# GpSimd's work in a diffusion layer moved to VectorE, behind ScalarE's rounding

## The chip, the core and the metric

One core of a Trainium2 chip runs the whole layer as one program. The metric is the device time of one execution in microseconds. The kernel before takes 2390.72 us, the median of 3 runs (2388.92 to 2391.03).

## The reference, cut to what matters

One layer of a hybrid diffusion backbone over 512 latent tokens and 256 context tokens, width 2048, everything in float32:

```
x  = x + grid_pos_embed
sh1, sc1, gt1, sh2, sc2, gt2 = split(silu(c) @ w_ada + b_ada)      # the ada matrix: 2048 x 12288
hx = rms_norm(x) * (1 + sc1) + sh1                                 # the same for the context, with c_ctx
u_f, u_x, u_g = split(hx @ w_in)
y_lru     = (forward + backward RG-LRU of conv(u_x)) * gelu(u_g)   # 8 heads of 128
y_fourier = real(fft2(u_f)) @ w_fourier + b                        # 4 groups of 256
x  = x + gt1 * rms_norm(concat(y_fourier, y_lru) @ w_out)
h2 = rms_norm(x) * (1 + sc2) + sh2
g, v = split(conv(h2 @ w_up))                                      # 2 x 5632 wide, 3 taps
x  = x + gt2 * rms_norm((gelu(g) * v) @ w_down)
```

## The kernel before

**Number format.** Activations and weights are cut in two parts so that float32 products can be made by three faster matmuls: hi is the value rounded to fp32r, lo is the value less hi. A product is hi x hi + hi x lo + lo x hi (`three`, L709 to L713).

**The weight stream.** All large weights come as 344 units of 128x1024 in the order of their use. A ring of four slots holds a unit three times: `w_raw` (what the DMA brought), `w_hi` (ScalarE, `round_unit`, L437 to L441) and `w_lo` (GpSimd, `remainders`, L391 to L396). Four units are a round. TensorE waits for `lo_done` before a unit. The semaphore `hi_done` counts ScalarE's roundings, and `lo_done` also frees `w_raw`: SP loads the next unit into a slot when the slot's last lo part is done (`load_unit`, L280). All loads go through SP's one queue, in the order of the code.

**The ada matrix.** The first 4096 columns are multiplied by TensorE at the start (L722 to L731, 0 to 135 us). The rest, 32 chunks of 256 columns, is worked out on VectorE beside the other work: `eat_ada` (L1017 to L1037) does one chunk as 16 steps `ada_acc = rows * scale + ada_acc` over 128x256, in pairs per load of 128x512, with four slots for the loads (`load_ada`, L288: a load waits until the slot was eaten). TensorE then sums `ada_acc` over the partitions (`sum_ada`, L779), and `take_ada` (L1011) adds the bias.

**The stages.** (1) TensorE's ada columns, the norms, and h in hi and lo (L1079 to L1106). (2) Eight heads (PE L787, ACT L499, DVE L1147): for head h TensorE makes u_x with units 0 and 1 of round h, and u_g with units 2 and 3, then the gates from `xc`. VectorE convolves, splits `xc`, takes the last ada chunk, finishes the head before, eats the next chunk, and works out the gap of the recurrence. ScalarE rounds units 0 and 1 of round h + 1 after the seeds of the convolution, and 2 and 3 after the exponentials. (3) Four Fourier groups (L871, L553, L1183), two ada chunks each. (4) The output projection, 16 tiles of two units (L908, L609, L1289); beside it one ada chunk per tile. After each tile ScalarE rounds two units of the next round. During the last half of this stage GpSimd adds the positions to x1 (eight additions of 128x1024, L405). (5) Between the halves: x1 is made from y (L1312 to L1319, 16 tiles: a scaling on VectorE, then a sum; GpSimd has 11 of the sums, in `POOL_SUM`), its squares are summed, h2 is made in hi and lo (L1323 to L1332; GpSimd has 5 of the 16 tiles, `POOL_H2`), and a last ada chunk but one is eaten. (6) The FFN in 11 chunks of 4 pairs: a pair is four units (g, then v), a down projection eight units; VectorE adds convolution taps (L1338, L1341), splits the activations (L1346), multiplies (L1358) and adds the down tiles (L1365). (7) The last norm and sum (L1396 to L1403; GpSimd has 11 of the 16 sums) and the stores.

**Who orders what.** Every engine has one list of instructions, written out by hand, and works through it in order. A wait stands in the list and holds back all that follows it on that engine. GpSimd's list has little beside `remainders`, so it stands waiting for `hi_done` and starts at once.

Of the kernel before, what the change touches and what calls it, by code (L numbers as in the profile page):

```python
# [21 lines left out]
F32 = mybir.dt.float32  # L22
# [7 lines left out]
KT = D // P  # L30
# [69 lines left out]
def build(nc, x_t, ctx_t, par_d, late_d, stream, ada0, adabg, gates_d, tabs_d, out_t):  # L100
    ctx = ExitStack()
    with ctx:
# [95 lines left out]
        with ExitStack() as s:  # L198
# [39 lines left out]
        y_normed, x1_done, x1_squared, x1_summed = (  # L238
            sem("y_normed"), (sem("x1_dve"), sem("x1_pool")), sem("x1_squared"), sem("x1_summed"))
        h2_pre, h2_rounded, h2_ready = ((sem(n + "_dve"), sem(n + "_pool")) for n in ("h2_pre", "h2_rounded", "h2_ready"))  # L240
# [4 lines left out]
        f_normed, out_ready, stored = sem("f_normed"), (sem("out_dve"), sem("out_pool")), sem("stored")  # L245
# [15 lines left out]

        POOL_SUM = [k for k in range(KT) if k % 3 != 2]
        POOL_H2 = [k for k in range(KT) if k % 3 == 2]

        def shared(sems, pool_tiles, k):

            mine = k in pool_tiles
            return sems[mine], sum((j in pool_tiles) == mine for j in range(k + 1))

# [9 lines left out]
        def _(sp):  # L279
# [103 lines left out]
            for k in range(KT):  # L383
                sp.wait_ge(*shared(out_ready, POOL_SUM, k))
                sp.dma_start(out_t[:, k, :], x1[:, k, :]).then_inc(stored, 16)
            sp.wait_ge(stored, 16 * KT)


        @block.gpsimd
        def _(pool):  # L390
            def remainders(r, slots=range(RING)):  # L391
                for s in slots:

                    pool.wait_ge(hi_done, r * RING + s + 1)
                    nc.gpsimd.tensor_tensor(w_lo[:, s, :], w_raw[:, s, :], w_hi[:, s, :].bitcast(F32),  # L395
                                            ALU.subtract).then_inc(lo_done, 1)  # L396

            with pool.Fori(0, R_OUT + 5) as r:
                remainders(r)

            pool.wait_ge(late_in, 16)
            for i in range(4):
                pool.wait_ge(x_in[i], 32)
                for half in range(2):
                    nc.gpsimd.tensor_tensor(*positions(x1, late_par, 4 * i + 2 * half, 2), ALU.add).then_inc(x_posed, 1)  # L405
                    if i + half < 4:
                        remainders(R_OUT + 5 + i, (2 * half, 2 * half + 1))

            for n, k in enumerate(POOL_SUM):
                pool.wait_ge(y_normed, n + 1)  # L410
                nc.gpsimd.tensor_tensor(x1[:, k, :], x1[:, k, :], tile(acc, k), ALU.add).then_inc(x1_done[1], 1)
            remainders(R_FFN, (2, 3))

            pool.wait_ge(rms_done, 4)
            for n in range(len(POOL_H2) + 1):
                if n < len(POOL_H2):
                    k = POOL_H2[n]
                    nc.gpsimd.tensor_tensor(tile(acc, k), x1[:, k, :], ss1[:, :], ALU.mult).then_inc(h2_pre[1], 1)
                if n > 0:
                    k = POOL_H2[n - 1]  # L420
                    pool.wait_ge(h2_rounded[1], n)
                    nc.gpsimd.tensor_tensor(h_lo[:, k, :], tile(acc, k), h_hi[:, k, :].bitcast(F32),
                                            ALU.subtract).then_inc(h2_ready[1], 1)
            with pool.Fori(R_FFN + 1, ROUNDS) as r:
                remainders(r)

            for n, k in enumerate(POOL_SUM):
                pool.wait_ge(f_normed, n + 1)
                nc.gpsimd.tensor_tensor(x1[:, k, :], x1[:, k, :], tile(acc, k), ALU.add).then_inc(out_ready[1], 1)
# [1073 lines left out]
```

## Time and profile before

| | us |
|---|---|
| median of 3 runs | 2390.72 |
| lowest, highest run | 2388.92, 2391.03 |
| profiled execution, span | 2397.1 |
| TensorE busy | 2224.0 |
| VectorE busy | 1170.5 |
| ScalarE busy | 717.5 |
| GpSimd busy | 918.3 |

The profile is of one execution of its own, and gives its span, from the first to the last instruction; its time isn't listed beside it, and the span stands 6.4 us above the median of the runs. PE is TensorE, DVE VectorE, ACT ScalarE, POOL GpSimd, SP the queue that issues the loads. Busy times of matmuls overlap, so a busy TensorE is not one at its peak. PEclk is the granted clock of TensorE as a share of 2.4 GHz; it has two levels, 2.4 and 1.2 GHz.

### The profile page before, as it was taken

To read this page: it belongs to the slowest core of one execution; us is meant where nothing else is said; L and a number is where in the kernel's file an instruction comes from. 1 tells how busy PE (TensorE), PEld (TensorE's weight loads), DVE (VectorE), ACT (ScalarE), POOL (GpSimd) and SP (SyncE) were. 2 spreads that over 40 slices of the span, in tenths; PEclk is the share of its full clock that TensorE was granted. 3 is DMA by queue.
4 is the path that set the end of the run, shared out by engine and by line. 5 is a ranking of instruction groups with operands and counts; after the bars stand their busy time and mean duration, and the time that the engine had idled before them with its cause. 6 is when DMAs were issued, how large, how long until landed. Compare 5 with 4: busy or idle time off the path is not lost.

```text
span 2397.1 us, 27540 instructions
## 1 busy us (share of the span) xinstructions
PE 2224.0 (93%) x9640; PEld 1750.7 (73%) x9640; DVE 1170.5 (49%) x1548; ACT 717.5 (30%) x938; POOL 918.3 (38%) x388
## 2 busy tenths in 40 slices
PE   8999989788888857999999999999999999999994
PEld 1268878677766626888888888888888888888883
DVE  4478888887788987323222222323232222223237
ACT  2345565422221233222222222222222222222222
POOL 0023222222234554444444444444444444444443
PEclk9999999888998978999999999999999999999997
DMA  9863424354476623323222222323232222223221
GB/s 347 277 206 112 148 82 142 134 169 145 137 249 231 210 75 105 105 88 103 90 97 96 95 97 88 104 87 105 88 101 91 96 96 93 99 88 104 87 87 70
DMA packets 102135, 301.50 MB, mean 126 GB/s; under 512 B 11344, under 2 KB 11344, under 8 KB 100816
## 3 DMA queue, kind: packets, MB, share of 16 engines
q1 hardware_dynamic: 102096, 300.99, 37.8%
q8 instruction: 23, 0.38, 0.1%
q14 instruction: 16, 0.13, 0.0%
HBM read 296.76 MB, written 4.19 MB: 126 GB/s over the span
## 4 chain that ended last, share of the span: by engine, by line
PE 69%; DVE 21%; DMA 5%; issue 3%; ACT 2%; DVEq 0%; POOL 0%; SPq 0%; ACTq 0%; POOLq 0%
PE bank L711 21%; PE bank L712 21%; PE bank L713 21%; DVE ada_acc L1033 10%; PE bank L729 4%; DMA ada_raw<-in_adabg 3%; DMA w_raw<-in_ada 1%; DVE xc L1120 1%; DVE ada_acc L1027 1%; DVE lru_i L1162 1%; DVE acc L1313 1%; DVE lru_i L1130 1%; DVE lru_u L1166 1%; DVE acc L1397 1%; DVE lru_u L1139 1%
## 5 line engine op out<-in xcount | busy, mean ns | idle before, releaser
L395 POOL TENSOR_TENSOR w_lo<-w_raw,w_hi 128x1024 fp32r<-128x1024 f32 x344 | 847.6, 2484 | 1411.0 <-ACT w_hi L441 1411.0
L711 PE MATMUL bank<-h_hi,w_hi 128*128 128x512 f32 x2048 | 814.4, 398 | 15.4 <-DVE h_lo L1331 9.4
L712 PE MATMUL bank<-h_lo,w_hi 128*128 128x512 f32 x2048 | 810.2, 396 | 0.0
L713 PE MATMUL bank<-h_hi,w_lo 128*128 128x512 f32 x2048 | 809.0, 395 | 0.0
L441 ACT ACTIVATE w_hi<-w_raw 128x1024 fp32r<-128x1024 f32 x344 | 347.5, 1052 | 1201.2 <-PE bank L713 1109.1
L711 PEld LDWEIGHTS bank<-h_hi,w_hi 128*128 128x128 f32 x2048 | 392.8, 192 | 94.0 <-issue 15.2
L713 PEld LDWEIGHTS bank<-h_hi,w_lo 128*128 128x128 f32 x2048 | 391.8, 191 | 83.7
L712 PEld LDWEIGHTS bank<-h_lo,w_hi 128*128 128x128 f32 x2048 | 392.8, 192 | 76.4
L1033 DVE SCALAR_TENSOR_TENSOR ada_acc<-ada_raw,csil,ada_acc 128x256 f32<-128x256 f32 x480 | 337.3, 703 | 42.7 <-DMA ada_raw<-in_adabg 23.4
L711 PE MATMUL bank<-act_hi,w_hi 128*128 128x512 f32 x704 | 278.5, 396 | 0.0
L712 PE MATMUL bank<-act_lo,w_hi 128*128 128x512 f32 x704 | 278.5, 396 | 0.0
L713 PE MATMUL bank<-act_hi,w_lo 128*128 128x512 f32 x704 | 278.5, 396 | 0.0
L1346 DVE TENSOR_TENSOR act_lo<-cg,act_hi 128x512 fp32r<-128x512 f32 x44 | 66.4, 1510 | 361.6 <-ACT act_hi L653 361.6
L1365 DVE TENSOR_TENSOR acc<-acc,bank 128x512 f32<-128x512 f32 x160 | 109.2, 687 | 268.7 <-PE bank L713 268.7
L1338 DVE SCALAR_TENSOR_TENSOR cv<-bank,late_par,cv 128x511 f32<-128x511 f32 x44 | 33.0, 749 | 343.2 <-ACT cv L649 343.2
L713 PEld LDWEIGHTS bank<-act_hi,w_lo 128*128 128x128 f32 x704 | 132.3, 188 | 32.0
L711 PEld LDWEIGHTS bank<-act_hi,w_hi 128*128 128x128 f32 x704 | 132.3, 188 | 31.9
L712 PEld LDWEIGHTS bank<-act_lo,w_hi 128*128 128x128 f32 x704 | 132.3, 188 | 31.9
L729 PE MATMUL bank<-w_raw,csil 128*2 128x512 f32 x256 | 116.2, 610 | 10.6 <-DMA w_raw<-in_ada 10.5
L729 PEld LDWEIGHTS bank<-w_raw,csil 128*2 128x2 f32 x256 | 21.0, 86 | 100.2 <-issue 70.7
L1358 DVE TENSOR_TENSOR cg<-cg,cv 128x512 f32<-128x512 f32 x44 | 85.4, 1940 | 1.5
L783 PE MATMUL bank<-par,ada_acc 128*128 128x1 f32 x128 | 20.3, 263 | 68.3 <-DVE ada_acc L1033 68.3
(188 smaller groups left out, 1577.5 us busy)
## 6 DMA issues: line engine op xcount, KB each, us to landing
w_raw<-in_stream SPq DMA_DIRECT2D x344, 512.0 KB, 3.4
ada_raw<-in_adabg SPq DMA_DIRECT2D x256, 256.0 KB, 3.7
w_raw<-in_ada SPq DMA_DIRECT2D x64, 512.0 KB, 4.6
x<-in_x_t SPq DMA_DIRECT2D x8, 1024.0 KB, 7.4
out_t<-x SPq DMA_DIRECT2D x16, 256.0 KB, 2.0
c<-in_ctx_t SPq DMA_DIRECT2D x2, 1024.0 KB, 7.9
g_raw<-in_gates SPq DMA_DIRECT2D x8, 256.0 KB, 4.3
y_four<-in_tabs SPq DMA_DIRECT2D x4, 258.0 KB, 4.8
```

Of the source, the lines that this page charges most:

```text
L395: nc.gpsimd.tensor_tensor(w_lo[:, s, :], w_raw[:, s, :], w_hi[:, s, :].bitcast(F32), ALU.subtract).then_inc(lo_done, 1)
L441: nc.scalar.activation(w_hi[:, s, :], w_raw[:, s, :], ACT.Copy).then_inc(hi_done, 1)
L711: nc.tensor.matmul(out, w, v, start=start, stop=False)
L712: nc.tensor.matmul(out, w, v_l, start=False, stop=False)
L713: return nc.tensor.matmul(out, w_l, v, start=False, stop=stop)
L729: mm = nc.tensor.matmul(bank[half][0:2, :], csil[:, 2 * k:2 * k + 2], w_raw[:, s, 512 * i:512 * i + 512], start=k == 0, stop=k == KT - 1)
L1027: ins = v.tensor_scalar(ada_acc[:, :], rows, scale, None, ALU.mult)
L1033: ins = v.scalar_tensor_tensor(ada_acc[:, :], rows, scale, ada_acc[:, :], ALU.mult, ALU.add)
L1338: chain.step(v.scalar_tensor_tensor(dst[:, 1:L], b[:, 0:L - 1], lcol(late_par, "ffn_conv_w", tile_no * 3, 1), dst[:, 1:L], ALU.mult, ALU.add))
L1346: v.tensor_tensor(act_lo[:, q, :], cg[:, q % 2, :], act_hi[:, q, :].bitcast(F32), ALU.subtract).then_inc(ffn_split, 1)
L1358: v.tensor_tensor(cg[:, p % 2, :], cg[:, p % 2, :], cv[:, :], ALU.mult).then_inc(ffn_prod, 1)
L1365: v.tensor_tensor(tile(acc, m), tile(acc, m), bank[4 + m % 4][:, :], ALU.add).then_inc(down_added, 1)
```

## The change

GpSimd's whole list is dropped. Its work goes into VectorE's list, each piece behind the rounding that it needs:

- in a head, units 0 and 1 after the split of `xc` and ahead of `take_ada`; units 2 and 3 at the end of the head, after the gap. Round 0 stands before the first head
- in a Fourier group, two units ahead of each `fourier_input`
- in the output projection, two units at the end of each tile; the position sums at the end of tile pairs 3 to 6. The loop over tile pairs is written out (a plain `for` in place of a loop on the engine)
- between the halves, all 16 sums and all 16 tiles of h2, the latter in one form, so ScalarE also loses its extra pass for 5 of them
- in the FFN, two units ahead of the split of the last activation, two between the two convolutions, and two after every fourth down tile
- the last 16 sums

The waits of ScalarE, TensorE and SP become plain counts. The core of the diff:

```
-        @block.gpsimd
-        def _(pool):
-            def remainders(r, slots=range(RING)):
...
 # vector
+            def remainders(rnd, *slots):
+                for s in slots:
+                    dve.wait_ge(hi_done, rnd * RING + s + 1)
+                    v.tensor_tensor(w_lo[:, s, :], w_raw[:, s, :], w_hi[:, s, :].bitcast(F32), ALU.subtract).then_inc(lo_done, 1)
...
                 v.tensor_tensor(xc_lo[:, :], xc[:, :], xc_hi[:, :].bitcast(F32), ALU.subtract).then_inc(xc_split, 1)
+                remainders(h + 1, 0, 1)
                 take_ada(h, bank[5])
...
                     v.scalar_tensor_tensor(lru_u[:, d, :], lru_r[:, d, :], 1.0, lru_u[:, d, :],
                                            ALU.add, ALU.mult).then_inc(gap_done, 1)
+                remainders(h + 1, 2, 3)
+
+            remainders(0, 0, 1, 2, 3)
             head(0)
...
                 n = g * 2 + t
+                remainders(g + R_FOUR + 1, 2 * t, 2 * t + 1)
                 dve.wait_ge(uf_copied, n + 1)
...
                     add_square(ss1[:, :], sq1[:, t, :], m + 2 * KT, first=first)
+                    if i < KT // 2 - 1 or t == 0:
+                        remainders(i + R_OUT + 1, 2 * t, 2 * t + 1)
+
+            def place(j):
+
+                dve.wait_ge(x_in[j], 32)
+                for half in range(2):
+                    v.tensor_tensor(*positions(x1, late_par, 4 * j + 2 * half, 2), ALU.add).then_inc(x_posed, 1)
 
             out_tiles(0)
-            with chain.loop(1, KT // 2 - 1, 16) as i:
+            dve.wait_ge(late_in, 16)
+            for i in range(1, KT // 2 - 1):
                 out_tiles(i)
-            dve.wait_ge(late_in, 16)
+                if i > 2:
+                    place(i - 3)
...
             for k in range(KT):
-                ins = v.scalar_tensor_tensor(tile(acc, k), tile(acc, k), gain_y[:, k:k + 1], ss1[:, :], ALU.mult, ALU.mult)
-                if k in POOL_SUM:
-                    ins.then_inc(y_normed, 1)
-                else:
...
+                chain.step(v.scalar_tensor_tensor(tile(acc, k), tile(acc, k), gain_y[:, k:k + 1], ss1[:, :], ALU.mult, ALU.mult))
+                chain.wait()
+                v.tensor_tensor(x1[:, k, :], x1[:, k, :], tile(acc, k), ALU.add).then_inc(x1_done, 1)
+            remainders(R_FFN, 2, 3)
             inverse_rms(3, ss1[:, :])
...
-            def pair(c, p):
+            def pair(c, p, rnd):
                 n = c * CH + p
+                remainders(rnd, 0, 1)
                 if not (isinstance(c, int) and n == 0):
                     split_act(n - 1, (p - 1) % CH)
                 dve.wait_ge(seed_g, n + 1)
                 convolve_ffn(bank[2 * (p % 2)], cg[:, p % 2, :], n, conv_g)
+                remainders(rnd, 2, 3)
                 dve.wait_ge(seed_v, n + 1)
...
                 for m in range(KT):
                     add_down(c - 1, m)
+                    if m % 4 == 3:
+                        j = m // 4
+                        remainders(r0 + 2 + j // 2, 2 * (j % 2), 2 * (j % 2) + 1)
```

## Rows read from the trace of the kernel before

**Rows 1.** The page of the whole execution: busy time of each engine.

```profile
PE 2224.0 (93%) x9640; PEld 1750.7 (73%) x9640; DVE 1170.5 (49%) x1548; ACT 717.5 (30%) x938; POOL 918.3 (38%) x388
```

**Rows 2.** Windows by stage: us; busy PE, PEld, DVE, ACT, POOL; PEclk; DMA; GB/s.

```profile
170.40:455.00 284.60, 263.39 (x1324) 223.63 (x1325) 238.90 (x308) 164.92 (x213) 77.10 (x31) 0.96 0.38 127
455.00:588.00 133.00, 112.67 (x582) 97.53 (x580) 104.28 (x199) 32.39 (x55) 34.50 (x15) 0.90 0.51 164
588.00:631.50 43.50, 32.49 (x154) 28.14 (x153) 34.99 (x67) 15.32 (x27) 10.34 (x5) 0.84 0.16 49
631.50:847.00 215.50, 178.69 (x729) 143.78 (x729) 185.87 (x254) 43.59 (x55) 85.12 (x35) 0.91 0.69 229
847.00:928.60 81.60, 45.84 (x134) 26.44 (x134) 71.97 (x66) 33.83 (x48) 48.77 (x27) 0.77 0.17 51
928.60:2340.00 1411.40, 1411.38 (x6156) 1157.78 (x6157) 401.37 (x451) 358.95 (x429) 624.85 (x254) 1.00 0.30 96
```

**Rows 3.** The page's groups: the split of a unit on GpSimd.

```profile
L395 POOL TENSOR_TENSOR w_lo<-w_raw,w_hi 128x1024 fp32r<-128x1024 f32 x344 | 847.6, 2484 | 1411.0 <-ACT w_hi L441 1411.0
```

**Rows 4.** Groups of VectorE by line and shape; the first of 120 to 929 us.

```profile
L1033 DVE SCALAR_TENSOR_TENSOR ada_acc<-ada_raw,csil,ada_acc 128x256 f32<-128x256 f32 x465 | 330.1, 710 | 41.7 <-DMA ada_raw<-in_adabg 23.4
...
L1130 DVE TENSOR_TENSOR lru_i<-lru_i,lru_u 128x768 f32<-128x768 f32 x16 | 15.0, 937 | 0.0
...
L1142 DVE TENSOR_TENSOR lru_u<-lru_u 128x512 f32<-128x512 f32 x8 | 5.5, 693 | 0.3
...
L1103 DVE SCALAR_TENSOR_TENSOR h_lo<-x,mod_x,h_hi 128x512 fp32r<-128x512 f32 x16 | 11.9, 743 | 0.0
```

**Rows 5.** Timeline of VectorE and GpSimd in one head: start, us, what.

```profile
288.08 7.23 DVE L1033 SCALAR_TENSOR_TENSOR ada_acc<-ada_raw,csil,ada_acc 128x256 f32<-128x256 f32 x6 [1.19 <-DMA ada_raw<-in_adabg]
...
288.51 4.95 POOL L395 TENSOR_TENSOR w_lo<-w_raw,w_hi 128x1024 fp32r<-128x1024 f32 x2 [14.58 <-ACT w_hi L441]
...
303.40 0.69 DVE L1150 TENSOR_TENSOR g_lo<-g_raw,g_hi 128x512 fp32r<-128x512 f32 x1 [1.43 <-ACT g_hi L504]
...
309.54 1.49 DVE L1155 TENSOR_TENSOR xc_lo<-xc,xc_hi 128x768 fp32r<-128x768 f32 x1 [0.91 <-ACT xc_hi L514]
```

**Rows 6.** Timeline around TensorE's first unit: TensorE, and VectorE's last part of h.

```profile
137.29 0.79 PE L711 MATMUL bank<-h_hi,w_hi 128*128 128x512 f32 x1 [0.58 <-POOL w_lo L395]
...
147.45 0.47 DVE L1105 SCALAR_TENSOR_TENSOR hc_lo<-c,mod_c,hc_hi 128x256 fp32r<-128x256 f32 x1
```

**Rows 7.** Timeline of VectorE in one Fourier group.

```profile
527.87 0.42 DVE L1193 TENSOR_TENSOR eo<-u_sb 128x255 f32<-128x255 f32 x1
...
538.25 3.09 DVE L1033 SCALAR_TENSOR_TENSOR ada_acc<-ada_raw,csil,ada_acc 128x256 f32<-128x256 f32 x6 [0.28 <-DMA ada_raw<-in_adabg]
...
547.82 2.62 DVE L1193 TENSOR_TENSOR eo<-u_sb 128x255 f32<-128x255 f32 x1
```

**Rows 8.** Waits in the output projection: us in total, times, longest.

```profile
PE bank L783 <- DVE ada_acc L1033: 43.0, 12, 6.4
...
DVE ada_acc L1033 <- DMA ada_raw<-in_adabg: 6.0, 5, 1.8
```

**Rows 9.** Timeline before the FFN: VectorE, and TensorE's wait.

```profile
914.49 14.08 DVE L1033 SCALAR_TENSOR_TENSOR ada_acc<-ada_raw,csil,ada_acc 128x256 f32<-128x256 f32 x15
...
928.62 0.59 PE L783 MATMUL bank<-par,ada_acc 128*128 128x1 f32 x2 [12.79 <-DVE ada_acc L1033]
```

**Rows 10.** Timeline of ScalarE and GpSimd inside the FFN.

```profile
1207.78 2.01 ACT L441 ACTIVATE w_hi<-w_raw 128x1024 fp32r<-128x1024 f32 x2 [8.99 <-PE bank L713]
...
1218.57 2.01 ACT L441 ACTIVATE w_hi<-w_raw 128x1024 fp32r<-128x1024 f32 x2 [7.60 <-PE bank L713]
...
1208.91 5.22 POOL L395 TENSOR_TENSOR w_lo<-w_raw,w_hi 128x1024 fp32r<-128x1024 f32 x2 [6.24 <-ACT w_hi L441]
```

**Rows 11.** Timeline of the last sums: the first and the last.

```profile
2369.23 3.08 DVE L1397 SCALAR_TENSOR_TENSOR acc<-acc,gain,ss 128x512 f32<-128x512 f32 x3
...
2393.37 1.26 POOL L429 TENSOR_TENSOR x<-x,acc 128x512 f32<-128x512 f32 x1 [1.29 <-DVE acc L1397]
```

More of the change, by code:

```diff
@@ L260, in build @@
         GATE_BANKS = ((3, 5), (6, 1))
[L262 to L268, printed above, removed]
         R_FOUR = U_HEADS // RING
@@ L383, in _ @@
             for k in range(KT):
-                sp.wait_ge(*shared(out_ready, POOL_SUM, k))
+                sp.wait_ge(out_ready, k + 1)
                 sp.dma_start(out_t[:, k, :], x1[:, k, :]).then_inc(stored, 16)
             sp.wait_ge(stored, 16 * KT)
-        @block.gpsimd
-        def _(pool):
-            def remainders(r, slots=range(RING)):
[L392 to L429, printed above, removed]
         @block.scalar
@@ L626, in _ @@
             for k in range(KT):
-                act.wait_ge(*shared(x1_done, POOL_SUM, k))
+                act.wait_ge(x1_done, k + 1)
                 if k > 1:
@@ L636, in _ @@
                 shift = mod_x[:, 3 * KT + k:3 * KT + k + 1]
-                act.wait_ge(*shared(h2_pre, POOL_H2, k))
-                if k in POOL_H2:
-                    chain.step(nc.scalar.activation(tile(acc, k), tile(acc, k), ACT.Identity,
-                                                    bias=shift, scale=gain_f[:, k:k + 1]))
-                    chain.wait()
-                    nc.scalar.activation(h_hi[:, k, :], tile(acc, k), ACT.Copy).then_inc(h2_rounded[1], 1)
-                else:
-                    nc.scalar.activation(h_hi[:, k, :], tile(acc, k), ACT.Identity, bias=shift).then_inc(h2_rounded[0], 1)
+                act.wait_ge(h2_pre, k + 1)
+                nc.scalar.activation(h_hi[:, k, :], tile(acc, k), ACT.Identity, bias=shift).then_inc(h2_rounded, 1)
             def seed(f, src, dst, tile, done):
@@ L951, in _ @@
                             k = 8 * half + j
-                            pe.wait_ge(*shared(h2_ready, POOL_H2, k))
+                            pe.wait_ge(h2_ready, k + 1)
                             for t, done in enumerate((up_g, up_v)):
@@ L1312, in _ @@
             for k in range(KT):
[L1313 to L1327 removed]
+                chain.step(v.scalar_tensor_tensor(tile(acc, k), tile(acc, k), gain_y[:, k:k + 1], ss1[:, :], ALU.mult, ALU.mult))
+                chain.wait()
+                v.tensor_tensor(x1[:, k, :], x1[:, k, :], tile(acc, k), ALU.add).then_inc(x1_done, 1)
+            remainders(R_FFN, 2, 3)
+            inverse_rms(3, ss1[:, :])
+            for n in range(KT + 1):
+                if n < KT:
+                    v.scalar_tensor_tensor(tile(acc, n), x1[:, n, :], gain_f[:, n:n + 1], ss1[:, :],
+                                           ALU.mult, ALU.mult).then_inc(h2_pre, 1)
                 if n > 0:
[L1329 to L1330 removed]
+                    k = n - 1
+                    dve.wait_ge(h2_rounded, n)
                     v.scalar_tensor_tensor(h_lo[:, k, :], tile(acc, k), mod_x[:, 3 * KT + k:3 * KT + k + 1],
[L1332 removed]
+                                           h_hi[:, k, :].bitcast(F32), ALU.add, ALU.subtract).then_inc(h2_ready, 1)
             eat_ada(FFN_ADA, 0, BGU)
@@ L1390, in _ @@
                 add_down(NCH - 1, m)
+                if m in (3, 7):
+                    remainders(ROUNDS - 1, m // 2 - 1, m // 2)
                 for j in range(2 * m - KT, 2 * m - KT + 2):
@@ L1396, in _ @@
             for k in range(KT):
-                ins = v.scalar_tensor_tensor(tile(acc, k), tile(acc, k), gain_d[:, k:k + 1], ss2[:, :], ALU.mult, ALU.mult)
-                if k in POOL_SUM:
-                    ins.then_inc(f_normed, 1)
-                else:
-                    chain.step(ins)
-                    chain.wait()
-                    v.tensor_tensor(x1[:, k, :], x1[:, k, :], tile(acc, k), ALU.add).then_inc(out_ready[0], 1)
+                chain.step(v.scalar_tensor_tensor(tile(acc, k), tile(acc, k), gain_d[:, k:k + 1], ss2[:, :], ALU.mult, ALU.mult))
+                chain.wait()
+                v.tensor_tensor(x1[:, k, :], x1[:, k, :], tile(acc, k), ALU.add).then_inc(out_ready, 1)
 def dft_tables():
```

28 lines of the change are left out of this document (7 added, 21 removed).

## The prediction

> **What bounds the kernel now.** I read the page first, for which engine is full: TensorE is busy 93% of the span and VectorE 49% [rows 1]. An average over unlike stages says little, so the windows by stage came next. Between 928.6 and 2340 us, the FFN, TensorE is busy 1411.38 of 1411.40 us at full clock: that stage is TensorE's, and VectorE has 1010 us to spare in it. In the five stages ahead TensorE's share falls (93%, 85%, 75%, 83%, 56%) and its granted clock with it, down to 0.77, while VectorE holds 84, 78, 80, 86 and 88% [rows 2]: there TensorE waits for VectorE in part of every period. So the change has to be priced in those stages, and at the start and the end.
>
> Then the groups and timelines, for what VectorE does there. Its ada step over 128x256 takes 0.50 us undisturbed (3.09 us for six, started 0.5 apart [rows 7]), yet the mean of 465 is 0.710 [rows 4]. The timeline of a head shows why: six steps take 7.23 us where six free ones take 3.1, while GpSimd does two units in 4.95 us [rows 5]. Two of the six lasted a whole GpSimd instruction. GpSimd's split of a unit, 2.484 us [rows 3], stops a VectorE instruction that reads two SBUF tensors, at about 2.0 us per meeting. Over the ada steps alone that is 330.1 - 465 x 0.50 = 98 us ahead of the FFN [rows 4]; the 255-column difference (2.62 for 0.42 us) and the split of xc (1.49 for 0.94) show the same [rows 4, 5, 7].
>
> **The moved work, each piece.** A unit is 128x1024, tensor_tensor. VectorE takes 0.693 us for 512 and 0.937 for 768 columns [rows 4], so some 0.25 us per 256 and 1.2 us for 1024; back to back an instruction starts about 0.07 before the last one ends, so I use 1.15. From outside: not under 0.94, nor over GpSimd's 2.48. Units before the FFN: 84 x 1.15 = 97 us; eight position sums at 1.2 make 10; eleven residual sums and ten h2 steps at 0.7 make 15. VectorE is given 122 us ahead of the FFN, and gets back the 98 above plus what the other instructions lose (I estimate 50 to 60, as one such instruction in each part of a head or group meets a unit). The balance is near -30, but the path decides:
>
> - **First units.** GpSimd now splits unit 0 while VectorE still makes h, and TensorE starts at 137.29. After, all four splits stand behind h, whose last part starts at 147.45 [rows 6]; without one meeting h ends at 145.9, one split gives 147.1. TensorE starts 9.8 us later, but waits less for h inside the unit and loses less to the half clock. Price +8 (between +5 and +12).
> - **Heads, seven periods of 36.8 us.** Added on the path: two splits between xc_lo and take_ada, +2.3; the other two fall into the 1.43 us wait for g_hi and its neighbours [rows 5], so +0.5 is left. Returned: xc_lo 0.55; in the ada steps 2 x 2.05 = 4.1 at most. Part of that is not gained: steps 5 to 8 wait for transfers that go out only as slots are eaten (1.19 us already [rows 5]). I take 2.1. Sum +0.1 per head, total 0 (from -14, all of it gained, to +16, none). TensorE's second job then waits some 2 us for its late splits; it has that room, as it waits 3.6 us for take_ada now. SP's unit loads wait for lo_done, now up to 10 us later in a head, but the ada load queued behind waits for the next head's steps anyway.
> - **Into Fourier:** the last finish_head loses two meetings (4.1), gets 2.3: -2.5.
> - **Fourier groups, three on the cycle.** +0.6 as the splits hold eo until ScalarE has rounded both units, +2.4 for those before the next input; -2.9 on the eo pair (3.9 to 0.8 us [rows 7]), -3.5 in the ada chunk. -3.4 each: -10 (-5 to -12).
> - **Turn to the output projection:** -2 on the last eo pair, and -5 in the first chunk, where TensorE waits.
> - **Output projection, 14 tile periods in 215.5 us [rows 2], 15.4 each.** TensorE waits 43.0 us for ada_acc [rows 8]. Now a tile is 8.2 of steps, 4.1 of meetings, 0.85 of sums, and some 2.2 of DMA wait, hops and the position sums' meetings. After: 8.2 + 0.8 + 2.3 of splits, and DMA wait with hops, which I put at 2.4 against some 1 now (6.0 in total inside the chunks [rows 8]), because steps that are not held up reach their slot earlier: 13.7, or 192 for 14, plus 9.6 of position sums: 201.5. Sum -14 (from -33, DMA as now, to +26: splits 32 and sums 10, less the position sums' eight meetings of 2.0).
> - **Between the halves (847 to 928.6).** The x1 sums run 16 x 1.4 = 22.5 instead of 25.5: -3; the two splits after them lie under ScalarE's root. h2 becomes 16 pairs of 0.743 [rows 4], 1.33 a pair back to back, all on VectorE: -3. The next ada chunk, 2.48 + 14.08 us long [rows 9], holds three to four meetings and TensorE waits 12.79 for it: -7, but TensorE then needs one split, +1.2. Less half clock after a shorter gap, -2. Sum -14 (-8 to -20).
> - **FFN.** 256 splits, 300 us of VectorE. Covered: a slot pair is rounded by 2.01 us and needed again 10.8 us after the round began (1207.78 to 1218.57), and GpSimd ends at 1214.1 [rows 10]; VectorE would end at +3.5, leaving 7 us. Queued behind its new wait for hi stand seed and product, needed a job later. Zero; if cover fails, each late microsecond is paid up to 44 times.
> - **Tail.** From 2369.23 to 2394.63 [rows 11], 25.4 us become 22.5: -3.
>
> Sum: 8 + 0 - 2.5 - 10 - 7 - 14 - 14 + 0 - 3 = -42.5. The profiled execution's span, 2397.1, becomes 2354.6. It stands 6.4 above the median of 2390.7, so I forecast 2348.
>
> **A rule that speaks against it.** The ada steps stretch to a GpSimd instruction's length whenever they meet one [rows 5]. The Trainium skill, page "Perfetto Trace Analysis", section "Optimizing Scalar/DVE Operations", says that where VectorE is saturated, giving some work to ScalarE or even GpSimd may make sense, and adds that between GpSimd and VectorE it may not help, since they share a read port. By the first half alone all 122 us would be added, to 2519; by the second the meetings must be set against it, as in the sum. The rows side with the second half.
>
> **Rivals.**
> - **A, the sum above** (0.56): -25 to -62.
> - **B, transfers don't hold the steps** (0.24). Heads gain 2 each (-14), the tiles run at 12.3 us (-33, 19 more than in the sum), so 2397.1 - 42.5 - 33 = 2321.6, median 2315. For it: in a Fourier chunk eight loads cost only 0.28 us of wait [rows 7]. Against: 229 GB/s are moved in the output stage already [rows 2].
> - **C, slower: VectorE pays and the ada transfers keep the return** (0.10). Chunks end when their last load lands, whether or not steps were blocked. Then every split on the path counts whole: heads +16, Fourier +1, turn and entry +4, output +26, between the halves -5, first units +8, tail -3: +47, median 2438. It decides from the point where a load takes over 4 x 1.04 us plus the time won. For it: 41.7 us of idle already precede the steps, 23.4 by DMA [rows 4]. Against: the run of six at 288.08 had no wait inside it [rows 5]. It is the first half of the skill's rule as a mechanism of this kernel.
> - **D, slower in the FFN** (0.03): in-order waits make TensorE wait a microsecond per pair, +44, which cancels the gain.
> - **E, nothing** (0.07 shared with mixtures of A and C).
>
> About 0.2% (5 us) is what a measurement of this kernel can tell from no change. Faster by more: A, B and part of the mixtures, 0.84; within: 0.04; slower: C and parts of D and E, 0.12. The range reaches from B's middle, 2316, to where C begins to mix in, 2386; about one in ten lies beyond either end.
>
> **What would show it.** GpSimd idle; VectorE's share 56 to 58%; the splits near 1.2 us; the ada step's mean 0.50 and the 255-column difference 0.42 wherever they run; product and act_lo down from their stretched length to 0.69. First unit's matmul near 147; FFN 1411 us at full clock; TensorE's waits for ada_acc in the output projection well under 43 us, VectorE's DMA waits there above 6. Wrong if splits take over 1.5 us, if the DMA waits ahead of the steps grow by the whole return (C), or if the FFN window is longer than 1411 us (D).

## The result, and the profile after

The changed kernel takes 2310.74 us (median of 4 runs, 2310.41 to 2313.72), the kernel before 2390.88 us beside it: ratio 0.9664, interval 0.965 to 0.9677. That is 80 us or 3.4% faster. I had forecast 2348 us with a range of 2316 to 2386: the direction was right, the size was not (5 us below the range), and what came true is rival B, whose middle was 2315. One of the ten executions of e7 below took 7192.85 us at a granted clock of 0.287, where the other nine took 2388 to 2397, and is left out of its figures.

First the page and VectorE's groups of the changed kernel, which answer to [rows 1, 3, 4]: busy time, then per group count, busy us, mean ns, and idle time before.

```profile
PE 2195.4 (95%) x9640; PEld 1729.8 (75%) x9640; DVE 1316.1 (57%) x1932; ACT 714.0 (31%) x933; POOL 0.2 (0%) x4
...
L1054 DVE TENSOR_TENSOR w_lo<-w_raw,w_hi 128x1024 fp32r<-128x1024 f32 x344 | 405.9, 1222 | 580.7 <-ACT w_hi L388 580.7
...
L974 DVE SCALAR_TENSOR_TENSOR ada_acc<-ada_raw,csil,ada_acc 128x256 f32<-128x256 f32 x480 | 232.8, 485 | 51.1 <-DMA ada_raw<-in_adabg 26.6
```

GpSimd is idle. VectorE does the same split in 1.222 us for which GpSimd took 2.484 [rows 3], and the ada step's mean has fallen from 0.710 [rows 4] to 0.485 us, the same in each stage: no step is held up any more. VectorE took on 384 instructions (1932 for 1548) and is busy only 145.6 us longer; its 344 splits alone are 406.

In the FFN the stretched instructions shrank as well. Groups of VectorE from 850 to 2250 us in the changed kernel:

```profile
L1315 DVE TENSOR_TENSOR cg<-cg,cv 128x512 f32<-128x512 f32 x44 | 30.5, 693 | 1.5
...
L1301 DVE TENSOR_TENSOR act_lo<-cg,act_hi 128x512 fp32r<-128x512 f32 x44 | 30.2, 686 | 0.7 <-ACT act_hi L594 0.7
```

Windows by stage of the changed kernel, which answer to [rows 2] (us; busy PE, PEld, DVE, ACT, POOL; PEclk; DMA; GB/s): heads, Fourier, the turn, output projection, between the halves, FFN.

```profile
178.00:430.00 252.00, 241.32 (x1270) 206.95 (x1269) 219.55 (x320) 157.94 (x205) 0.00 (x0) 1.00 0.38 132
430.00:560.00 130.00, 115.80 (x615) 100.18 (x614) 109.41 (x228) 37.29 (x61) 0.00 (x0) 0.93 0.56 184
560.00:597.00 37.00, 33.20 (x177) 28.76 (x176) 30.09 (x71) 15.97 (x30) 0.00 (x0) 0.95 0.27 83
597.00:775.00 178.00, 167.83 (x724) 136.56 (x724) 154.31 (x288) 43.09 (x55) 0.00 (x0) 0.96 0.82 276
775.00:850.00 75.00, 52.31 (x151) 31.20 (x152) 69.88 (x98) 32.52 (x46) 0.00 (x0) 0.82 0.21 64
850.00:2250.00 1400.00, 1400.00 (x6119) 1148.34 (x6118) 596.88 (x701) 357.94 (x427) 0.00 (x0) 1.00 0.30 97
```

TensorE's share rose in the heads from 93% to 96% and in the output projection from 83% to 94%, its granted clock there from 0.96 to 1.00 and from 0.91 to 0.96. The output stage now moves 276 GB/s where it moved 229 [rows 2]: the transfers had that much in reserve. The FFN is as it was, TensorE's alone. Taken from the first head to TensorE's sum ahead of the FFN (177.7 to 843.5 us), VectorE is busy 577.1 of 665.8 us, where it was busy 636.0 of 758.2 in the five windows of [rows 2]: 59 us less work, for which the prediction had a balance near -30, and 33 us less idling.

One head of the changed kernel, VectorE's timeline, which answers to [rows 5]:

```profile
283.86 4.65 DVE L974 SCALAR_TENSOR_TENSOR ada_acc<-ada_raw,csil,ada_acc 128x256 f32<-128x256 f32 x9
289.52 1.01 DVE L974 SCALAR_TENSOR_TENSOR ada_acc<-ada_raw,csil,ada_acc 128x256 f32<-128x256 f32 x2 [1.01 <-DMA ada_raw<-in_adabg]
291.42 2.05 DVE L974 SCALAR_TENSOR_TENSOR ada_acc<-ada_raw,csil,ada_acc 128x256 f32<-128x256 f32 x4 [0.89 <-DMA ada_raw<-in_adabg]
...
300.03 2.35 DVE L1054 TENSOR_TENSOR w_lo<-w_raw,w_hi 128x1024 fp32r<-128x1024 f32 x2
302.30 0.68 DVE L1097 TENSOR_TENSOR g_lo<-g_raw,g_hi 128x512 fp32r<-128x512 f32 x1
302.90 3.96 DVE L1067 SCALAR_TENSOR_TENSOR xc<-bank,par,xc 128x510 f32<-128x510 f32 x6
307.78 0.96 DVE L1102 TENSOR_TENSOR xc_lo<-xc,xc_hi 128x768 fp32r<-128x768 f32 x1 [0.91 <-ACT xc_hi L461]
308.65 2.36 DVE L1054 TENSOR_TENSOR w_lo<-w_raw,w_hi 128x1024 fp32r<-128x1024 f32 x2
```

Six steps that took 7.23 us [rows 5] now take 3.06 of work with 0.89 of DMA wait inside. The late pair of splits ends where g_lo used to wait 1.43 us for ScalarE [rows 5]; there is no wait left there, so part of it is free, as forecast. The split of xc is back to 0.96 us.

Waits in the output projection of the changed kernel (600 to 779 us; total, times, longest), which answer to [rows 8]:

```profile
DVE ada_acc L974 <- DMA ada_raw<-in_adabg: 7.0, 11, 1.7
...
PE bank L652 <- DVE w_lo L1054: 6.4, 7, 1.1
...
PE bank L724 <- DVE ada_acc L974: 3.8, 6, 1.6
```

TensorE's wait for ada_acc went from 43.0 to 3.8 us, and 6.4 us of waits for VectorE's splits came in its place. VectorE's own wait for transfers inside the chunks went from 6.0 only to 7.0 us. This is the number that decides between A and B. Two further waits belong beside it, ahead of a chunk's first step and for TensorE's sum. Before (631.5 to 847 us):

```profile
DVE mod_x L1015 <- PE bank L783: 8.9, 13, 2.5
DVE ada_acc L1027 <- DMA ada_raw<-in_adabg: 6.6, 4, 3.2
```

And after:

```profile
DVE ada_acc L968 <- DMA ada_raw<-in_adabg: 2.5, 2, 1.3
DVE mod_x L956 <- PE bank L724: 0.6, 1, 0.6
```

So all DMA waits of this stage together are 12.6 us before (7.9 in e7's execution, described below) and 9.5 after, and the splits stand where VectorE used to wait 8.9 us for TensorE. The other stages show the same. From the first head to the FFN the DMA waits in the ada steps are 29.6 us before (22.3 in e7's) and 27.6 after, while three waits that the splits now fill have all but gone: 10.0 us of g_lo for ScalarE in the heads, 15.7 of the eo inputs for ScalarE in the Fourier groups, 9.4 for TensorE's sums; 4.6 us of waiting for ScalarE's roundings came in their place.

The other places: TensorE's first unit [rows 6], and its gap ahead of the FFN [rows 9].

```profile
146.26 0.80 PE L652 MATMUL bank<-h_hi,w_hi 128*128 128x512 f32 x1 [10.41 <-DVE w_lo L1054]
...
843.55 1.01 PE L724 MATMUL bank<-par,ada_acc 128*128 128x1 f32 x4 [4.03 <-DVE ada_acc L974]
```

And VectorE and ScalarE: the 255-column difference in a Fourier group [rows 7], an unbroken ada chunk there, the one ahead of the FFN [rows 9], and a pair of roundings in the FFN with the splits behind it [rows 10].

```profile
506.87 0.42 DVE L1143 TENSOR_TENSOR eo<-u_sb 128x255 f32<-128x255 f32 x1
...
512.66 7.85 DVE L974 SCALAR_TENSOR_TENSOR ada_acc<-ada_raw,csil,ada_acc 128x256 f32<-128x256 f32 x15
...
835.24 8.25 DVE L974 SCALAR_TENSOR_TENSOR ada_acc<-ada_raw,csil,ada_acc 128x256 f32<-128x256 f32 x15
...
1210.23 2.01 ACT L388 ACTIVATE w_hi<-w_raw 128x1024 fp32r<-128x1024 f32 x2 [8.11 <-PE bank L654]
...
1211.33 2.36 DVE L1054 TENSOR_TENSOR w_lo<-w_raw,w_hi 128x1024 fp32r<-128x1024 f32 x2 [0.51 <-ACT w_hi L388]
```

The FFN's splits end 3.46 us after the round began (1213.69 less 1210.23), as forecast.

**Where the time went.** I put eight marks in both timelines, all but the last at the start of an instruction: the last one of the first head's y_lru, the first and the last eo input of the Fourier groups, the first and the last acc copy of the output projection, the second product of the FFN, the last root, the end. The third column takes, in place of the kernel before, the same kernel with its tile loop written out (e7 below), whose time is the same but whose profiled execution, 2386.6 us, lies nearer to its median.

| stage | forecast | before to after | e7 to after |
|---|---|---|---|
| start, to the first y_lru | +8 | +6.7 | +10.5 |
| heads, and into Fourier | -2.5 | -17.6 | -16.6 |
| Fourier groups | -10 | -14.2 | -13.1 |
| turn | -7 | -5.0 | -4.9 |
| output projection | -14 | -37.1 | -34.4 |
| between the halves, to the second product | -14 | -17.1 | -14.3 |
| FFN | 0 | -0.6 | -1.6 |
| tail | -3 | -3.1 | -3.0 |
| sum | -42.5 | -88.0 | -77.4 |

The runs say -80, so the profiled execution of before had some 8 us too many and e7's some 3 too few, and the third column is the fairer one. (In every execution listed with both, the time stands 1.8 us above the span; 2397.1 is then 8 us too long, where the prediction took 6.4.) By either the miss has two places: the heads and the output projection.

### The profile page after: what moved, and what is told of

It reads as the page before. It is cut to its first block, busy times and chain, and to the rows that moved or that the text cites. A ratio compares the mean times of both kernels' runs of the same rounds, so it can differ in the third digit from the quotient of the medians.

```text
span 2309.1 us, 27081 instructions
## 1 busy us (share of the span) xinstructions
PE 2195.4 (95%) x9640; PEld 1729.8 (75%) x9640; DVE 1316.1 (57%) x1932; ACT 714.0 (31%) x933; POOL 0.2 (0%) x4
## 4 chain that ended last, share of the span: by engine, by line
PE 71%; DVE 18%; DMA 6%; issue 3%; ACT 1%; DVEq 0%; SPq 0%; ACTq 0%
PE bank L652 22%; PE bank L653 22%; PE bank L654 22%; DVE ada_acc L974 5%; DMA ada_raw<-in_adabg 4%; PE bank L670 4%; DVE w_lo L1054 3%; DMA w_raw<-in_ada 1%; DVE xc L1067 1%; DVE lru_i L1077 1%; DVE lru_u L1114 1%; DVE lru_i L1110 1%; DVE x L1276 0%; DVE x L1362 0%; DVE acc L1360 0%
## 5 line engine op out<-in xcount | busy, mean ns | idle before, releaser
L1054 DVE TENSOR_TENSOR w_lo<-w_raw,w_hi 128x1024 fp32r<-128x1024 f32 x344 | 405.9, 1222 | 580.7 <-ACT w_hi L388 580.7
L652 PEld LDWEIGHTS bank<-h_hi,w_hi 128*128 128x128 f32 x2048 | 389.0, 190 | 127.1 <-DVE w_lo L1054 37.1
L974 DVE SCALAR_TENSOR_TENSOR ada_acc<-ada_raw,csil,ada_acc 128x256 f32<-128x256 f32 x480 | 232.8, 485 | 51.1 <-DMA ada_raw<-in_adabg 26.6
L559 ACT ACTIVATE acc<-bank 128x512 f32 (+1 forms) x16 | 9.6, 598 | 105.1 <-PE bank L654 105.1
L1067 DVE SCALAR_TENSOR_TENSOR xc<-bank,par,xc 128x511 f32<-128x511 f32 (+3 forms) x48 | 28.8, 614 | 14.5 <-ACT xc L457 11.9
L1296 DVE SCALAR_TENSOR_TENSOR cg<-bank,late_par,cg 128x511 f32<-128x511 f32 x44 | 33.0, 750 | 6.8 <-DVE cg L1293 2.6
L654 PE MATMUL bank<-hc_hi,w_lo 128*128 128x256 f32 x128 | 36.7, 287 | 0.0
```

The lines of the kernel that those rows point to most:

```text
L652: nc.tensor.matmul(out, w, v, start=start, stop=False)
L654: return nc.tensor.matmul(out, w_l, v, start=False, stop=stop)
L974: ins = v.scalar_tensor_tensor(ada_acc[:, :], rows, scale, ada_acc[:, :], ALU.mult, ALU.add)
L1054: v.tensor_tensor(w_lo[:, s, :], w_raw[:, s, :], w_hi[:, s, :].bitcast(F32), ALU.subtract).then_inc(lo_done, 1)
L1067: ins = v.scalar_tensor_tensor(dst, b[:, lo + off:hi + off], w, dst, ALU.mult, ALU.add)
L1296: v.scalar_tensor_tensor(dst[:, 0:L - 1], b[:, 1:L], lcol(late_par, "ffn_conv_w", tile_no * 3 + 2, 1), dst[:, 0:L - 1], ALU.mult, ALU.add) ...
```

## The experiments

Ten kernels ran, each beside the kernel before on the same chip. Two theories stood against each other at first, with a third beside them. **M**: what is won is the time for which a GpSimd instruction that reads SBUF holds up VectorE's two-input instructions; it comes back whole, since transfers don't hold the steps. **N**: the gain lies in something else that the change did, the order of the work, plain waits, or the loop written out, and the meetings matter little. **T**: a split takes 1.22 instead of 2.48 us, so that units and slots come free earlier.

### e1 and e2: GpSimd given something to do beside the changed kernel

```
+            pool.wait_ge(h_ready, KT)
+            n = 0
+            for r in range(1, R_FFN):
+                for s in range(RING):
+                    pool.wait_ge(hi_done, r * RING + s + 1)
+                    for _ in range(4):
+                        if n:
+                            pool.wait_ge(beside, n)
+                        nc.gpsimd.tensor_tensor(spare[:, :], par[:, 0:256], par[:, 0:256], ALU.add).then_inc(beside, 1)   # e1
+                        nc.gpsimd.memset(spare[:, :], 0.0).then_inc(beside, 1)                                            # e2
+                        n += 1
```

> The changed kernel, with work added on GpSimd that nothing waits for: at each rounding of rounds 1 to 19 (the heads, the Fourier groups, the output projection) four sums of 128x256 whose inputs are two reads of one resident tensor, into a spare tensor. VectorE's list is untouched. Theory M (the return of the change is that VectorE's two-input instructions no longer meet GpSimd's reads): the meetings come back though no split is on GpSimd. Each unit's four sums take some 2.5 us together and stop VectorE for up to 2 us; 76 units, of which VectorE is at work on two-input instructions for most, as its own splits now start at the same moment: 60 to 130 us slower than the changed kernel, the ada step's mean over 0.60 instead of 0.485. Theory T (the return is that a split takes 1.22 instead of 2.48 us, so that units and slots come free earlier): nothing here delays a split's release, within 3 us of the changed kernel and the ada step at 0.485.

> The changed kernel, with the same instructions in the same places on GpSimd as in the run with reads, but fills that only write 128x256 and read nothing. Theory M: VectorE's second input has no rival, so no meeting, within 3 us of the changed kernel (2311), the ada step at 0.485. A rival to M, that any work of GpSimd beside VectorE holds it up (its writes, or its waits and counts): slower, by a share of the run with reads that follows the busy time.

e1 takes 2370.5 us (ratio 0.9915, 0.9899 to 0.9932), e2 2308.91 us (0.9667, 0.9648 to 0.9687). Sums that no other work needs (ScalarE waits for them once, at the end of the output projection, 6 us after the last has ended) took away 60 of the 80 us; memsets at the same places took nothing. Groups on the page of e1:

```profile
L391 POOL TENSOR_TENSOR spare<-par 128x256 f32<-128x256 f32 x304 | 251.2, 826 | 564.5 <-ACT w_hi L403 542.2
L990 DVE SCALAR_TENSOR_TENSOR ada_acc<-ada_raw,csil,ada_acc 128x256 f32<-128x256 f32 x480 | 261.6, 545 | 45.9 <-DMA ada_raw<-in_adabg 20.8
```

The same on the page of e2:

```profile
L990 DVE SCALAR_TENSOR_TENSOR ada_acc<-ada_raw,csil,ada_acc 128x256 f32<-128x256 f32 x480 | 232.7, 485 | 52.2 <-DMA ada_raw<-in_adabg 27.7
...
L391 POOL MEMSET spare<- 128x256 f32 x304 | 96.1, 316 | 657.7 <-ACT w_hi L403 641.5
```

With memsets the ada step stays at 485 ns, with sums it is 545. That is less than the 600 expected, and its 480 steps make 29 of the 60 us; over all its instructions VectorE is busy 67 us longer than in the changed kernel (1383.5 for 1316.1). The memsets are shorter (96 us of GpSimd for 251), but by busy time alone they would have cost some 23 us. So it is not GpSimd's activity but its reading that costs, and since e1 leaves every split on VectorE (mean 1.26 us), T doesn't explain these 60 us. The Trainium skill, page "SBUF — State Buffer", section "Who interferes with whom", says that a VectorE instruction with two SBUF inputs contends with a GpSimd instruction that reads SBUF and not with one that only writes it; these two runs agree with both halves, 60 us against none. What the page doesn't say is a price, and this kernel's is told by the rows above.

### e3 and e4: the FFN alone, one way and the other

e3 is the changed kernel with the FFN's units on GpSimd, e4 the kernel before with them on VectorE. The traces count 260 such units, not the 256 of the prediction and the expectations.

```
 e3, against after
-                remainders(rnd, 0, 1)        # in pair; likewise (2, 3), and behind the down tiles
+            with pool.Fori(R_FFN + 1, ROUNDS) as r:
+                remainders(r)
 e4, against before: the same lines the other way round
```

> The changed kernel with the FFN's 256 units split on GpSimd again, all that stands before the FFN as in the change. Both theories, and step 'FFN zero' of the prediction: TensorE is the bound there and covers either engine, so within 3 us of the changed kernel, 2308 to 2314, the FFN stage at full clock. If VectorE's in-order waits had cost or saved anything there, it would show as a difference of up to a microsecond a pair, 44.

> The kernel before with only the FFN's 256 units on VectorE, everything ahead on GpSimd as before. Expected within 3 us of the kernel before, 2388 to 2394: the meetings that vanish there (product and act_lo of a pair stretched to 1.94 and 1.51 us) are covered by TensorE. The sum of this one's and the other half's differences should give the whole change, -80.

Both miss. e3 takes 2322.87 us (0.9713, 0.9697 to 0.9729), 12 above the change where I allowed 3; e4 takes 2381.51 us (0.9965, 0.9951 to 0.9979), 8 below before. Their differences from before, 67 and 8, add up to 75 of the 80. From the second product to the last root e3 has 1406.6 us, e4 1405.9 and the changed kernel 1405.9: the FFN's steady part costs nothing either way. What differs is the stretch from the last h_lo to the second product: 47.45 us in e3 for 41.05 in the changed kernel, and 40.2 in e4 for 47.86 in the kernel before. (The first two count from the start of the last two h_lo, which stand in one row there, the other two from the last alone; compare only within a pair.) So the four units of the first FFN round are no part of the FFN: GpSimd splits them while VectorE eats the ada chunk between the halves. e9 and e10 test this.

### e9 and e10: only those four units moved

```
 e9, against e3
+                if isinstance(c, int) and n == 0:
+                    remainders(rnd, 0, 1)        # (2, 3) likewise, between the convolutions
-            with pool.Fori(R_FFN + 1, ROUNDS) as r:
+            pool.wait_ge(lo_done, (R_FFN + 2) * RING)
+            with pool.Fori(R_FFN + 2, ROUNDS) as r:
```

> The changed kernel with the FFN's 256 units split on GpSimd again, but for the four of the first FFN round, which stay on VectorE. GpSimd starts with the second round, so it can't meet the ada chunk between the halves. Giving all 256 back cost 12 us where 3 at most were expected (e3), and the stretch from the last h_lo to the second product was 47.45 us there against 41.05 in the changed kernel. If those four units are the cause of that stretch, it comes back to 41 to 42 us, and the kernel takes 2313 to 2319 us; what is then left above 2310.7 is the drift of some 5 us ahead of the FFN that e3 showed and that GpSimd, idle there, can't have made. If the stretch stays near 47 us, meetings in the first pairs of the FFN or the order of the loads are the cause, and the time stays at 2321 to 2325 us.

> The same kernel as e3, beside e9 on one chip, so that the difference of a few us is not one of chips. Both theories expect 2319 to 2325 us; if the 5-us drift ahead of the FFN in e3 was chance, it is 2316 to 2319 us and the last acc copy falls at 774 to 776 us after the span's start instead of 782.

e10, which is e3 again, takes 2320.5 us (0.9714, 0.9696 to 0.9732), e9 2307.82 us (0.9661, 0.9641 to 0.9681), which the intervals can't tell from the change itself (0.9664) and which lies 5 us below the range expected. Timeline of VectorE behind the last h_lo in e10:

```profile
836.19 0.35 DVE L979 TENSOR_SCALAR ada_acc<-ada_raw,csil 128x256 f32<-128x256 f32 x1
836.57 16.14 DVE L985 SCALAR_TENSOR_TENSOR ada_acc<-ada_raw,csil,ada_acc 128x256 f32<-128x256 f32 x15
```

And in e9:

```profile
829.35 0.35 DVE L980 TENSOR_SCALAR ada_acc<-ada_raw,csil 128x256 f32<-128x256 f32 x1
829.74 8.26 DVE L986 SCALAR_TENSOR_TENSOR ada_acc<-ada_raw,csil,ada_acc 128x256 f32<-128x256 f32 x15
```

Four GpSimd splits make fifteen steps 7.9 us longer, 2.0 each, as the prediction had read it off a head. The stretch to the second product is 46.8 us in e10 and 40.0 in e9, so 6.8 us of the difference are shown; the medians are 12.7 apart, the two profiled executions 14.6. Most of the rest lies ahead of it, 3.0 us before the last acc copy and 3.8 between that copy and the last h_lo, where VectorE has the same list in both. The first split of e10's GpSimd starts at 836.51, so no meeting made it; in e10 the last ada chunk of the output projection has a DMA wait of 1.25 us and ends 2.0 us after that copy, in e9 it ends 0.9 before it. I can't say what makes that: e3 and e10 are the same program, and their last acc copies lie 7.8 us apart (782.16 and 774.41), so the drift that I had read from e3 was chance, but the medians of the two kernels do differ by the whole 12.7.

With e9 the other 256 units of the FFN are priced: on GpSimd or on VectorE, no difference that the intervals show.

### e5 and e6: one stage given back to GpSimd

```
 e5
-                remainders(h + 1, 0, 1)
...
-                remainders(h + 1, 2, 3)
-            remainders(0, 0, 1, 2, 3)
+            with pool.Fori(0, R_FOUR + 1) as r:
+                remainders(r)
...
+            dve.wait_ge(lo_done, (R_FOUR + 1) * RING)
 e6
-                    if i < KT // 2 - 1 or t == 0:
-                        remainders(i + R_OUT + 1, 2 * t, 2 * t + 1)
+            pool.wait_ge(lo_done, (R_OUT + 1) * RING)
+            with pool.Fori(R_OUT + 1, R_FFN) as r:
+                remainders(r)
+            remainders(R_FFN, (0, 1))
...
+            dve.wait_ge(lo_done, R_FFN * RING + 2)
```

> The changed kernel with the units of rounds 0 to 8 (before and in the heads) split on GpSimd again. By the markers of the two traces the change costs 6.7 us up to the first head, gains 2.4 a head in six periods (14.2) and 5.7 in the last head's end, so without it the kernel should be 13 slower: 2324, between 2318 and 2330. If the heads' gain were due to something else in the trace (first stage, loads), it stays near 2311.

> The changed kernel with the output projection's units (rounds 13 to 20) split on GpSimd again, the position sums left on VectorE and the loop written out. The markers give 37 us for this stage and 5 for its entry. Theory M: most of it goes, 2335 to 2352, TensorE again waits for ada_acc. If the gain of the stage came from the loop written out or from the position sums' place, it stays within 8 us of 2311.

e5 takes 2317.8 us (0.9695, 0.9678 to 0.9712): 7 above the change where M said 13, just under the edge of what was expected. The last instruction of its first y_lru starts at 207.38 us (214.56 in the changed kernel), so GpSimd is worth 7.2 us at the start, and its heads then take 12.9 us more (last y_lru 452.41 for 446.67; the marks of the table let one expect 14.2 + 5.7 = 19.9), so moving the heads is worth 13 and costs 7 at the entry. Head by head the period is 36.3 us with GpSimd (207.38 to 425.13 over six) and 34.4 without.

The miss lies in the last head. From the seventh y_lru to the eighth are 27.3 us in e5, 31.4 in the kernel before and 25.7 in the changed one. In the kernel before GpSimd splits two units of the next round there, which e5 left on VectorE, and two scans meet them (timeline of VectorE and GpSimd, before):

```profile
452.99 2.87 DVE L1136 TENSOR_TENSOR_SCAN lru_u<-lru_r,lru_i 128x256 f32<-128x256 f32 x1
455.90 3.19 DVE L1139 TENSOR_TENSOR_SCAN lru_u<-lru_r,lru_u,lru_i 128x512 f32<-128x512 f32 x1
...
452.92 5.09 POOL L395 TENSOR_TENSOR w_lo<-w_raw,w_hi 128x1024 fp32r<-128x1024 f32 x2 [11.44 <-ACT w_hi L441]
```

In e5 the two scans take 0.69 and 1.28 us, 4.1 less.

e6 takes 2342.13 us (0.9801, 0.9786 to 0.9816), 31 above the change, as M said. Groups of e6 from 600 to 815 us:

```profile
L987 DVE SCALAR_TENSOR_TENSOR ada_acc<-ada_raw,csil,ada_acc 128x256 f32<-128x256 f32 x215 | 152.6, 710 | 19.3 <-DMA ada_raw<-in_adabg 4.6 <-DVE ada_acc L987 0.9
...
L384 POOL TENSOR_TENSOR w_lo<-w_raw,w_hi 128x1024 fp32r<-128x1024 f32 x29 | 72.8, 2510 | 134.1 <-ACT w_hi L401 134.1
```

Its waits in the same stretch:

```profile
PE bank L737 <- DVE ada_acc L987: 37.3, 12, 6.2
DVE ada_acc L987 <- DMA ada_raw<-in_adabg: 4.6, 6, 1.2
DVE ada_acc L981 <- DMA ada_raw<-in_adabg: 4.5, 3, 1.9
```

This is the run that settles the size. The steps are back at 710 ns, 225 above the changed kernel's 485, which makes 215 x 0.225 = 48 us; TensorE waits 37.3 us for ada_acc again. And VectorE's DMA waits are 9.1 us in all, beside 7.0 and 2.5 in the changed kernel: held up or not, the steps wait for transfers equally long. So nothing of the return went into waiting, where the prediction had assumed that much of it would. The 30 splits that VectorE is spared in e6 (30 x 1.15 = 34.5 us) don't make up for it. If all of them had stood on the path, the meetings would cost some 66 us in this stage with the 31 us of the result (an estimate, and an upper one, since part of the splits fills waits), 48 of them in the ada steps.

### e7: the loop written out

```
-            with chain.loop(1, KT // 2 - 1, 16) as i:
+            for i in range(1, KT // 2 - 1):
```

> The kernel before with VectorE's loop over tile pairs of the output projection written out, and nothing else. All theories of the splits: no difference, 2388 to 2394. If the register waits of the loop had held VectorE up, up to 0.3 us in each of 12 tiles, 4 us faster.

2391.26 us, ratio 1.0009 (0.9997 to 1.0021): no difference, so the loop is no part of the gain. e1 keeps the order of the work and the plain waits of the changed kernel and still loses 60 of the 80 us, so N can't be the main part. No run changes the order or the plain waits alone, and none gives the Fourier groups or the residual sums back to GpSimd alone: the runs that give one part back show 7 (e5), 31 (e6) and 10 to 12 us (e3, e10) of the 80.

### e8: GpSimd where it meets nobody

The convolution's taps take one input from PSUM and only one tensor from SBUF (`xc<-bank,par,xc`). In e8 GpSimd splits round 0 and, in each head, units 0 and 1 of the next round, which ScalarE rounds during the convolution; all else stays on VectorE.

```
-                remainders(h + 1, 0, 1)
...
+                dve.wait_ge(lo_done, h * RING + RING + 2)
                 remainders(h + 1, 2, 3)
-            remainders(0, 0, 1, 2, 3)
...
+            remainders(0)                            # GpSimd
+            with pool.Fori(1, R_FOUR + 1) as r:
+                pool.wait_ge(lo_done, r * RING)
+                remainders(r, (0, 1))
```

> The changed kernel with GpSimd splitting round 0 and units 0 and 1 of each head's next round again, units 2 and 3 and all the rest on VectorE. GpSimd's pair then falls beside the convolution, which reads PSUM and one SBUF tensor and kept its 3.96 us beside GpSimd in the kernel before, so it meets only the split of xc (0.55 us). Theory M: TensorE starts 9 us earlier and the first head gets 4 to 7 of it, a head's period loses 2.35 of splits, gains 0.55, until TensorE's own 33 us bind: 1.0 to 1.8 in each of 7 periods. Together 10 to 18 faster than the change, 2293 to 2301. If not VectorE but TensorE's wait for its late splits sets the heads, 4 to 7 from the start alone, 2304 to 2307.

2291.86 us (0.9595, 0.9582 to 0.9608): 19 us faster than the change and 98 faster than before, and a little below the 2293 that M allowed. Timeline of VectorE and GpSimd in a head of e8:

```profile
293.64 3.95 DVE L1080 SCALAR_TENSOR_TENSOR xc<-bank,par,xc 128x510 f32<-128x510 f32 x6
...
298.50 1.50 DVE L1115 TENSOR_TENSOR xc_lo<-xc,xc_hi 128x768 fp32r<-128x768 f32 x1 [0.91 <-ACT xc_hi L474]
...
294.42 4.78 POOL L384 TENSOR_TENSOR w_lo<-w_raw,w_hi 128x1024 fp32r<-128x1024 f32 x2 [27.68 <-ACT w_hi L401]
```

The window of its heads:

```profile
178.00:422.00 244.00, 237.81 (x1251) 203.95 (x1249) 211.50 (x307) 157.97 (x203) 33.38 (x14) 1.00 0.39 138
```

The six taps take 3.95 us with GpSimd beside them and 3.96 without. Only the tail of GpSimd's second unit catches the split of xc, 1.50 for 0.96 us. The period of a head is 32.6 us (208.49 to 404.04 over six) for 34.4, and TensorE is busy in 97% of the stretch at full clock: the heads have become TensorE's. Entry and heads give 17 of the 19 us, 6 of them up to the first y_lru (208.49 for 214.56). It shows too that the transfers could still follow at 32.6 us a head.

## Why the prediction came out as it did

- **What bounds the kernel, and the price of a meeting: right.** 2.0 us per meeting, read from [rows 5], is what e10 and e9 show (7.9 us for four). The ada step undisturbed is 0.485 us, I had 0.50 for steps started back to back; splits 1.222 for 1.2, the 255-column difference 0.42, position sums 1.219 us (eight).
- **First units, +8: right.** +6.7 or +10.5 by the two columns, and e5 says 7.2.
- **Heads, sum +0.1 each: wrong.** Failed was the term "Returned ... I take 2.1": of the 4.1 us per head, 2.0 were written off because "steps 5 to 8 wait for transfers that go out only as slots are eaten". In the heads' window (178 to 430 us) VectorE's DMA waits in the steps are 11.3 us before (9.3 in e7's execution) and 12.4 after: 0.15 to 0.4 us more a head, not 2.0. The period fell from 36.5 (e7) or 36.8 to 34.4 us, that is -2.1 to -2.4 each, as rival B had it, and -13 to -14 over the six periods between the marks. The rows hinted at it: in [rows 5] the one wait of 1.19 us stands ahead of the run of six, which has none inside, and the two meetings lie in that run, behind the last wait. What is won there could only be lost to loads that had landed under the held-up steps; in the head shown of after a wait of 0.89 us stands inside the last six, and the fifteen steps take 9.6 us from first to last where they took 13.1, so 3.5 of the 4.1 came back. I quoted that very row against rival C and didn't use it for the sum.
- **Into Fourier -2.5, turn -7: about right.** From the seventh y_lru to the first eo input 33.9 us became 30.5, so -3.4 for the last head and the entry where -2.4 was forecast; the turn gave -5.0.
- **Fourier groups, -10: mechanism right, a little small** (-13 to -14, where my own bounds were -5 to -12). A whole chunk runs unbroken now, 15 steps in 7.85 us. VectorE's 15.7 us of waiting for ScalarE's u_sb are gone, since one of a group's two pairs of splits stands there, as its price of +0.6 had it. No run gives the Fourier groups back alone, so which term was too small stays open.
- **Output projection, -14: wrong, the largest miss.** Failed was the term "DMA wait with hops, which I put at 2.4 against some 1 now". From the second acc copy to the last (595.32 to 774.68) there are 14 tiles in 179.4 us, or 12.1 each after 9.75 us of position sums. Work is 8.2 + 0.7 + 2.3 = 11.2, so DMA wait and hops are 0.9, not 2.4. The 1.6 us between my 13.7 and 12.1 make 22 us over 14 tiles. The term had a second fault: it let the hops stand, and the splits fill them (8.9 us of waiting for TensorE's sums before, 0.6 after). e6 shows the same from the other side: in this stage the DMA waits don't depend on whether the steps are held up (9.1 us for 9.5). My argument against B was that 229 GB/s were already moved here; the stage now moves 276. A rate that a stage has is not a limit that it has reached.
- **Between the halves, -14: right** (-14.3 by e7's execution, -17.1 by before's). The ada chunk fell from 14.08 to 8.25 us, TensorE's gap from 12.79 to 4.03.
- **FFN, 0: right.** TensorE is busy 1400.00 of 1400.00 us. Two flaws of counting: the FFN has 260 splits, not 256, and my expectations of e3 and e4 put the first FFN round with the FFN, while its four units met the ada chunk between the halves (e3, e4, e9, e10). The prediction had counted these meetings in the right place.
- **Tail, -3: right.**
- **The rule that speaks against the change** (the Trainium skill, page "Perfetto Trace Analysis", section "Optimizing Scalar/DVE Operations"). By its first half alone the time would have been 2519 us as the prediction has it (2513, with the 6.4 us taken off as in the other sums), and C, its mechanism here, 2438; the second half, that moving work between GpSimd and VectorE may not help, was too mild for this kernel. Here the move helped by 80 us, since one GpSimd split of 2.48 us took 2.0 from VectorE and the same split costs VectorE 1.2.
- **Chances.** B had 0.24. With the wait in [rows 5] read rightly it would have been the likeliest case, and A its pessimistic bound.

## What to carry to other kernels

When VectorE is short of time, GpSimd, whose reads hold it up, is no help by default: price a unit on GpSimd by what it takes from VectorE (here 2.0 us for one of 2.48) against what VectorE would take for it (1.2). Then look for the stretches where VectorE reads PSUM, or where another engine waits for the first unit, and put GpSimd there alone: that was worth another 19 us. Place the work that VectorE takes over where its list has waits for other engines anyway, as the 35 us of such waits here. And before writing a gain off to transfers, look where in the run their waits stand: what is won behind the last wait is mostly kept.

## What the runs showed that I had not expected

- 304 GpSimd sums of 0.83 us, which read SBUF, cost 60 us, and 304 memsets of 0.32 us in their places, which only write, cost nothing.
- Not only instructions with two tensors are held up. In e1 the first step of an ada chunk, a tensor_scalar with one tensor input, has a mean of 438 ns beside GpSimd's sums (26 of them, 178 to 800 us), for 348 in the changed kernel. The Trainium skill, page "SBUF — State Buffer", section "Who interferes with whom", allows for this: it counts tensor_scalar among the instructions that can take both port pairs. e1 shows the slowdown, not its cause.
- Two profiled executions of one program (e3 and e10) can lie 7.8 us apart at one mark in their middle, with medians 2.4 us apart. A drift of that size in one trace is no finding.
